# A softmax denominator's folded sum, split into a high and a low half and multiplied with ones in two rounded products

## The chip, the cores and the metric

The kernel runs on one core of one Trainium2 chip. The metric is the time of one execution on the device, in microseconds (us); a run's figure is the median of its executions. The engines are PE (TensorE, matrix products), DVE (VectorE), ACT (ScalarE), POOL (GpSimd) and SP (SyncE, which issues transfers).

## The reference, cut to what matters

An encoder layer. Its first attention path has 8 query heads in 2 groups of 4, sweeps all 2048 keys, and is an ordinary softmax:

```
s = jnp.einsum('bkgqd,bksd->bkgqs', qblk, k).astype(jnp.float32) * scale
p = jax.nn.softmax(s, axis=-1).astype(v.dtype)
return jnp.einsum('bkgqs,bksd->bkgqd', p, v)
```

For each query the kernel needs the weighted sum of the values and the sum of the 2048 exponentials, the denominator. Around it lie the input projection (stage 1), a windowed attention (3), the output projection (4) and a feed-forward net (5, 6).

## The kernel before, in words

The six stages run one after the other, each a block of its own with a barrier at its end. Stage 2, `attend_global` (L476 to L817), is the one that the change is in. It runs over 32 **groups** n: 8 heads times 4 chunks of 512 queries. A group is cut into 8 **units** u of 256 keys. Products use the rounded 32-bit type F32R, and where precision is needed a value is split in a rounded high part and a low rest. In the trace a unit is this:

- PE, `scores` (L766, L767): four products fill two of the four banks of `s_ps`; units alternate between the two pairs of banks, so `scores(u)` waits until DVE has finished the low part of unit u-2. Then `max_products` (L749) for the next group: two products into `m_ps`, which wait for DVE's last reduction. Then `weigh` (L781, L790) for unit u-2: two products with the high part, two with the low part. Unit 7 is also summed on PE (L784).
- ACT, `exponentials` (L676, L677): `p_hi`, the rounded exponential, and then the unrounded one in place.
- DVE, `low` (L720): `p_lo` = unrounded less rounded, for unit u-1; then `reduce` (L704): the running maximum for the next group. At u = 4 the eighth reduction of a group is followed by L708 and L711, which make the negated maximum `neg_max`.
- POOL: adds `p_hi` of units 0 to 6 up into `p_sum`, 128x1024 (L644, six adds), then folds the two halves of 512 together (L648). After the add of u = 4 it also runs `combine` for the group before (L630 and L634, 64x512 each), which puts two parts of the output together.

The order on each engine is the order of the program text, written out by hand; nothing is planned at run time. `total(n - 1)` (L794 to L796) is what turns the folded `p_sum` into the denominator: one product with the constant `ones_high`, in plain fp32, into a spare row of `ob_ps` of the group that runs then. PE issues it at the end of u = 4 of group n:

```
if u == 4 and n > 0:
    total(n - 1, False)
```

After the last group `total(31)` stands alone and ends the stage, followed by a copy on ACT (L697) and the stores. `ob_ps` itself is copied out by ACT in `keep_b` (L665) after u = 1 of the next group, `oa_ps` by `keep_a` (L658).

Semaphores of a stage can be used again by later stages. Those of stage 1 are collected in a list, `scratch["project_sems"]`, and POOL clears them one by one at the start of stage 4 (L1335, L1336); it then waits for the first `scale_heads` (L1347).

Of the kernel before, what the change touches and what calls it, by code (L numbers as in the profile page):

```python
# [21 lines left out]
F32 = mybir.dt.float32  # L22
F32R = mybir.dt.float32r
# [4 lines left out]
P = 128  # L28
# [103 lines left out]
def project(nc, a, scratch):  # L132
    with ExitStack() as ctx:
# [35 lines left out]
        qk_ps = ps("qk_ps", [P, 12, P])  # L169

        def sem(name):
            scratch["project_sems"].append(ctx.enter_context(nc.semaphore(name)))
            return scratch["project_sems"][-1]

        const_in = sem("const_in")
        gains_in = sem("gains_in")
# [299 lines left out]
def attend_global(nc, a, scratch):  # L476
# [11 lines left out]
    ADDS = BY_ADDS  # L488
    ONE_LOW, ONE_HIGH = HD, HD + 32
    with ExitStack() as ctx:  # L490
        sb, ps, sem = make_alloc(nc, ctx)
        kt = sb("kt", [P, NG, 2, SEQ], F32R)
        v = sb("v", [P, NT, NG, 2 * HD], F32R)
        v_one = sb("v_one", [P, NT, NG, 2 * HD], F32R)
# [10 lines left out]
        o_down = sb("o_down", [P, 2, QB])  # L505
        o_half = sb("o_half", [P, QB])
        o_sum = sb("o_sum", [P, 2, QB])
        ones_high = sb("g_ones_high", [P, 2 * HD])
        ones_low = sb("g_ones_low", [P, 2 * HD], F32R)
        s_ps = ps("s_ps", [P, 4, NB])  # L510
        m_ps = ps("m_ps", [P, 2, NB])
# [12 lines left out]
        scores_ready, p_hi_ready, probs_ready = sem("g_scores_ready"), sem("g_p_hi_ready"), sem("g_probs_ready")  # L524
        p_lo_ready, added = sem("g_p_lo_ready"), sem("g_added")
        high_used, low_used, sum_used = sem("g_high_used"), sem("g_low_used"), sem("g_sum_used")
        oa_kept, ob_kept = sem("g_oa_kept"), sem("g_ob_kept")
        shifted = [sem(f"g_shifted{s}") for s in range(2)]
        summed = sem("g_summed")
# [82 lines left out]
        @block.gpsimd  # L612
        def _(pool):
            nc.gpsimd.memset(kt[HD:HD + 1, :, 1, :].bitcast(F32), 1.0).then_inc(filled, 1)
            pool.drain()
            nc.gpsimd.memset(v_one[:, :, :, HD:ONE_HIGH].bitcast(F32), 1.0)
            pool.drain()
            nc.gpsimd.memset(v_one[:, :, :, ONE_HIGH:].bitcast(F32), 0.0).then_inc(filled, 1)
            pool.drain()
            nc.gpsimd.memset(ones_high[:, 0:ONE_HIGH], 0.0)  # L620
            pool.drain()
            nc.gpsimd.memset(ones_high[:, ONE_HIGH:], 1.0)
            nc.gpsimd.memset(ones_low[:].bitcast(F32), 0.0)
            pool.drain()
            nc.gpsimd.memset(ones_low[:, ONE_LOW:ONE_HIGH].bitcast(F32), 1.0).then_inc(filled, 1)

            def combine(n):
                s = n % 2
                pool.wait_ge(shifted[s], 16 * (n // 2 + 1))
                nc.gpsimd.tensor_tensor(o_half[0:HD], o_a[0:HD, s], o_down[0:HD, s], ALU.add)  # L630
                pool.wait_ge(ob_kept, n + 1)
                at_least(pool, o_stored[s], 16 * (n // 2))
                pool.drain()
                nc.gpsimd.tensor_tensor(o_sum[0:HD, s], o_half[0:HD], o_b[0:HD, s], ALU.add).then_inc(summed, 1)  # L634

            for n in range(TOTAL):
                s = n % 2
                for u in range(1, BY_ADDS):
                    pool.drain()
                    if u == 1:  # L640
                        at_least(pool, sum_used, n - 1)
                    pool.wait_ge(p_hi_ready, UNITS * n + u + 1)
                    first = p_hi[:, (UNITS * n) % SLOTS].bitcast(F32) if u == 1 else p_sum[:, s]
                    nc.gpsimd.tensor_tensor(p_sum[:, s], first, p_hi[:, (UNITS * n + u) % SLOTS].bitcast(F32), ALU.add).then_inc(added, 1)  # L644
                    if u == 4 and n > 0:
                        combine(n - 1)
                pool.drain()
                nc.gpsimd.tensor_tensor(p_sum[:, s, 0:QB], p_sum[:, s, 0:QB], p_sum[:, s, QB:], ALU.add).then_inc(added, 1)  # L648
            combine(TOTAL - 1)

        @block.scalar
        def _(act):
            def keep_a(n):
                s = n % 2
                act.wait_ge(high_used, UNITS * (n + 1))
                at_least(act, summed, n - 1)
                at_least(act, shifted[s], 16 * (n // 2))
                nc.scalar.activation(o_a[:, s], oa_ps[:], ACT.Copy).then_inc(oa_kept, 1)  # L658

            def keep_b(n):  # L660
                s = n % 2
                act.wait_ge(low_used, UNITS * (n + 1))
                at_least(act, summed, n - 1)
                at_least(act, den_stored[s], 32 * (n // 2) - (16 if s == 0 else 0) if n > 1 else 0)
                nc.scalar.activation(o_b[:, s], ob_ps[:], ACT.Copy).then_inc(ob_kept, 1)  # L665

            def exponentials(n, u):
                at = UNITS * n + u
                slot = at % SLOTS
                scored = s_ps[:, 2 * (u % 2):2 * (u % 2) + 2].rearrange("p b c -> p (b c)")  # L670
                act.wait_ge(scores_ready, at + 1)
                at_least(act, high_used, at - SLOTS + 1)
                before = at - SLOTS
                if at >= SLOTS and before % UNITS < BY_ADDS:
                    act.wait_ge(added, ADDS * (before // UNITS) + max(before % UNITS, 1))
                nc.scalar.activation(p_hi[:, slot], scored, ACT.Exp).then_inc(p_hi_ready, 1)  # L676
                nc.scalar.activation(scored, scored, ACT.Exp).then_inc(probs_ready, 1)  # L677

            def copy_v(g):
                act.wait_ge(v_loaded[g], 16)  # L680
                nc.scalar.activation(v_one[:, :, g, 0:HD], v[:, :, g, 0:HD].bitcast(F32), ACT.Copy).then_inc(v_copied, 1)

            copy_v(0)
            for n in range(TOTAL):
                for u in range(UNITS):
                    if u == 4 and n % ITER == ITER - 2 and n // ITER + 1 < NG:
                        copy_v(n // ITER + 1)
                    exponentials(n, u)
                    if u == LAG - 1 and n > 0:
                        keep_a(n - 1)  # L690
                        keep_b(n - 1)
            keep_a(TOTAL - 1)
            keep_b(TOTAL - 1)
            act.wait_ge(sum_used, TOTAL)
            act.wait_ge(den_stored[TOTAL % 2], 32 * (TOTAL // 2) - 16)
            act.wait_ge(summed, TOTAL - 1)
            nc.scalar.activation(o_b[:, TOTAL % 2], ob_ps[:], ACT.Copy).then_inc(ob_kept, 1)  # L697

        @block.vector
        def _(dve):  # L700
            def reduce(n, m):
                products = first_bank(m) if n == 0 else m_ps[:]
                dve.wait_ge(max_product, PAIRS * n + m + 1)
                nc.vector.tensor_reduce(part_max[:, m // (PAIRS // QT), m % (PAIRS // QT):m % (PAIRS // QT) + 1],  # L704
                                        products.rearrange("p b c -> p (b c)"), AX, ALU.max).then_inc(max_reduced, 1)
                if m == PAIRS - 1:
                    nc.vector.drain()
                    nc.vector.tensor_reduce(row_max[:], part_max[:], AX, ALU.max)  # L708
                    nc.vector.drain()
                    at_least(dve, max_placed[n % 2], 16 * QT * (n // 2))  # L710
                    nc.vector.tensor_scalar(neg_max[:, n % 2], row_max[:], -1.0, None, ALU.mult).then_inc(max_ready, 1)  # L711

            def low(n, u):
                at = UNITS * n + u
# [11 lines left out]
            for n in range(TOTAL):  # L726
                for u in range(UNITS):
                    if n > 0 or u > 0:
                        low(n if u else n - 1, (u - 1) % UNITS)
                    ahead, m = pair_of(n, u)  # L730
                    if ahead < TOTAL:
                        reduce(ahead, m)
            low(TOTAL - 1, UNITS - 1)

        @block.tensor
        def _(pe):
# [55 lines left out]
                last.then_inc(low_used, 1)  # L792

            def total(n, alone):  # L794
                pe.wait_ge(added, ADDS * (n + 1))
                nc.tensor.matmul(ob_ps[:], ones_high[:], p_sum[:, n % 2, 0:QB], start=alone, stop=alone).then_inc(sum_used, 1)  # L796

            for m in range(PAIRS):
                max_products(0, m)
# [3 lines left out]
            for n in range(TOTAL):  # L803
                for u in range(UNITS):
                    at = UNITS * n + u
                    scores(n, u)
                    ahead, m = pair_of(n, u)
                    if ahead < TOTAL:
                        max_products(ahead, m)
                    if at >= LAG:  # L810
                        weigh((at - LAG) // UNITS, (at - LAG) % UNITS)
                    if u == 4 and n > 0:
                        total(n - 1, False)
            for u in range(UNITS - LAG, UNITS):
                weigh(TOTAL - 1, u)
# [405 lines left out]
def mix_heads(nc, a, scratch):  # L1221
    with ExitStack() as ctx:
# [109 lines left out]

        @block.gpsimd
        def _(pool):
            for done in scratch["project_sems"]:  # L1335
                pool.sem_clear(done)  # L1336
            nc.gpsimd.memset(half[:], -0.5)
            pool.drain()
# [590 lines left out]
def build(nc, a, out, upto=6, kind="Internal"):  # L1929
    def dram(name, shape):  # L1930
        return nc.dram_tensor(name, shape, F32, kind=kind).ap()

    scratch = {
        "project_sems": [],
        "q_t": dram("q_turned", [HEADS // 2, P, SEQ]),
        "k_t": dram("k_turned", [NG, P, SEQ]),
        "v_glob": dram("v_glob", [NT, P, NG, 2 * HD]),
# [62 lines left out]
```

## Time and profile before

| what | value |
|---|---|
| median of 3 runs | 2890.35 us (2888.19 to 2890.84) |
| the profiled execution: its own time | 2890.22 us |
| the profiled execution: its span, first to last instruction | 2888.6 us |
| busy in the span: PE, DVE, ACT, POOL | 2705.4, 1827.9, 1429.2, 803.3 us |
| stage 2: its groups run | about 372 to 1046 us of the span |
| granted PE clock, mean | 0.972 of full speed (1.00 in the groups of stage 2) |

The profile is of one execution. Busy time is the time in which an engine had an instruction running; an instruction that is held up by another engine after it was started counts as busy. "Idle before" names the instruction that ended an engine's wait, as inferred from semaphores. The span leaves out 1.6 us around the first and the last instruction.

### The profile page before, as it was taken

How to read it: one execution, taken by the hardware profiler on the slowest of the kernel's cores; microseconds unless marked ns; L12 is line 12 of the kernel's file. 1: busy time of each engine (PE TensorE's matmuls, PEld its weight loads, DVE VectorE, ACT ScalarE, POOL GpSimd, SP SyncE). 2: the span in 40 equal slices, each digit the busy share in tenths (PEclk: the TensorE clock that was granted, in tenths of full speed). 3: DMA queues.
4: the chain of work that ended last, by engine and by line, in shares of the span. 5: the costliest groups of instructions: out<-in, count | busy, mean ns of one | idle time of the engine just before them, and what ended most of it. 6: DMA issues, size and time to landing. Idle time of an engine off the chain costs nothing. (4 is left out here: it accounts for less than half of the span.)

```text
span 2888.6 us, 36041 instructions
## 1 busy us (share of the span) xinstructions
PE 2705.4 (94%) x12274; PEld 2185.6 (76%) x12274; DVE 1827.9 (63%) x2503; ACT 1429.2 (49%) x2122; POOL 803.3 (28%) x603
## 2 busy tenths in 40 slices
PE   7999599999999978988995999999998999999998
PEld 5888467777777747976874888788886888888887
DVE  5666499999999947865556666675653343343433
ACT  3222177777777747973334544554443333233332
POOL 1111178888888854541110000000000000000000
PEclk9999799999999989998997999999999999999999
DMA  5333421111111122327876333533325445355442
GB/s 181 107 108 102 122 67 30 31 34 28 35 30 32 23 75 70 84 67 218 207 202 216 124 117 97 209 107 100 114 92 189 171 172 182 121 196 179 172 172 98
DMA packets 295611, 338.16 MB, mean 117 GB/s; under 512 B 73059, under 2 KB 219635, under 8 KB 293292
## 3 DMA queue, kind: packets, MB, share of 16 engines
q1 hardware_dynamic: 269980, 317.92, 35.7%
q10 hardware_dynamic: 23552, 13.64, 1.5%
q0 software_dynamic: 1936, 4.74, 0.6%
q8 instruction: 84, 1.38, 0.2%
q14 instruction: 59, 0.48, 0.0%
HBM read 234.10 MB, written 97.86 MB: 115 GB/s over the span
## 5 line engine op out<-in xcount | busy, mean ns | idle before, releaser
L126 PE MATMUL d_pr<-d_w_hi,d_s_hi 128*128 128x512 f32 x1024 | 399.7, 390 | 11.6 <-DVE d_s_lo L1872 11.6
L1871 DVE TENSOR_TENSOR d_w_lo<-d_w_raw,d_w_hi 128x1024 fp32r<-128x1024 f32 x128 | 156.8, 1225 | 386.2 <-ACT d_s_hi L1848 382.3
L127 PE MATMUL d_pr<-d_w_lo,d_s_hi 128*128 128x512 f32 x1024 | 399.5, 390 | 0.0
L128 PE MATMUL d_pr<-d_w_hi,d_s_lo 128*128 128x512 f32 x1024 | 399.3, 390 | 0.0
L644 POOL TENSOR_TENSOR p_sum<-p_sum,p_hi 128x1024 f32<-128x1024 f32 x160 | 383.3, 2396 | 37.0 <-issue 19.7
L126 PE MATMUL u_pr<-u_t_hi,u_w_hi 128*128 128x512 f32 x896 | 351.2, 392 | 32.3 <-DVE u_t_lo L1687 31.9
L127 PE MATMUL u_pr<-u_t_lo,u_w_hi 128*128 128x512 f32 x896 | 350.1, 391 | 0.0
L128 PE MATMUL u_pr<-u_t_hi,u_w_lo 128*128 128x512 f32 x896 | 350.1, 391 | 0.0
L676 ACT ACTIVATE p_hi<-s_ps 128x1024 fp32r<-128x1024 f32 x256 | 263.3, 1028 | 157.0 <-PE s_ps L767 155.7
L720 DVE TENSOR_TENSOR p_lo<-s_ps,p_hi 128x1024 fp32r<-128x1024 f32 x256 | 312.5, 1221 | 29.5 <-ACT s_ps L677 22.3
L704 DVE TENSOR_REDUCE part_max<-m_ps 128x1 f32<-128x1024 f32 x251 | 304.6, 1214 | 33.1 <-PE m_ps L749 32.9
L1846 ACT ACTIVATE d_w_hi<-d_w_raw 128x1024 fp32r<-128x1024 f32 x128 | 135.6, 1060 | 271.0 <-PE d_pr L128 181.3
L677 ACT ACTIVATE s_ps<-s_ps 128x1024 f32<-128x1024 f32 x256 | 261.4, 1021 | 0.0
L766 PE MATMUL s_ps<-q_all,kt 128*128 128x512 f32 x512 | 219.1, 428 | 18.3 <-DVE p_lo L720 18.2
L126 PEld LDWEIGHTS d_pr<-d_w_hi,d_s_hi 128*128 128x128 f32 x1024 | 192.9, 188 | 52.2 <-DVE d_s_lo L1872 12.1
L128 PEld LDWEIGHTS d_pr<-d_w_hi,d_s_lo 128*128 128x128 f32 x1024 | 193.0, 188 | 40.2
L127 PEld LDWEIGHTS d_pr<-d_w_lo,d_s_hi 128*128 128x128 f32 x1024 | 193.0, 188 | 40.0
L126 PEld LDWEIGHTS u_pr<-u_t_hi,u_w_hi 128*128 128x128 f32 x896 | 169.2, 189 | 70.4 <-issue 34.4
L1630 ACT ACTIVATE u_pr<-u_pr 128x512 f32<-128x512 f32 x128 | 74.5, 582 | 273.4 <-DVE u_pr L1716 126.7
L767 PE MATMUL s_ps<-q_max,kt 65*128 65x512 f32 x512 | 203.9, 398 | 0.0
L1839 POOL TENSOR_TENSOR d_rstd<-d_var,d_half 128x1 f32<-128x1 f32 x16 | 8.8, 550 | 699.7 <-DVE d_var L1879 699.7
L127 PEld LDWEIGHTS u_pr<-u_t_lo,u_w_hi 128*128 128x128 f32 x896 | 169.3, 189 | 35.2
(219 smaller groups left out, 5384.5 us busy)
## 6 DMA issues: line engine op xcount, KB each, us to landing
d_w_raw<-in_w_ffn_down SPq DMA_DIRECT2D x128, 512.0 KB, 3.8
u_w_raw<-in_w_ffn_up SPq DMA_DIRECT2D x32, 1024.0 KB, 6.0
act_blocks<-u_s_out SPq DMA_DIRECT2D x128, 256.0 KB, 6.2
d_s_lo<-act_blocks SPq DMA_DIRECT2D x128, 256.0 KB, 2.7
u_t_lo<-h_blocks SPq DMA_DIRECT2D x14, 1024.0 KB, 10.9
x_in<-in_x SPq DMA_DIRECT2D x16, 512.0 KB, 4.3
q_split<-q_out ACTq DMA_DIRECT2D x16, 512.0 KB, 3.3
q_turned<-w_raw SPq DMA_DIRECT2D x16, 512.0 KB, 3.4
```

The lines of the kernel that those rows point to most:

```text
L126: nc.tensor.matmul(out, stat_hi, mov_hi, start=first, stop=False)
L127: nc.tensor.matmul(out, stat_hi, mov_lo, start=False, stop=False)
L128: return nc.tensor.matmul(out, stat_lo, mov_hi, start=False, stop=last)
L644: nc.gpsimd.tensor_tensor(p_sum[:, s], first, p_hi[:, (UNITS * n + u) % SLOTS].bitcast(F32), ALU.add).then_inc(added, 1)
L676: nc.scalar.activation(p_hi[:, slot], scored, ACT.Exp).then_inc(p_hi_ready, 1)
L677: nc.scalar.activation(scored, scored, ACT.Exp).then_inc(probs_ready, 1)
L704: nc.vector.tensor_reduce(part_max[:, m // (PAIRS // QT), m % (PAIRS // QT):m % (PAIRS // QT) + 1], products.rearrange("p b c -> p (b c)") ...
L720: nc.vector.tensor_tensor(p_lo[:, slot], scored, p_hi[:, slot].bitcast(F32), ALU.subtract).then_inc(p_lo_ready, 1)
L766: nc.tensor.matmul(bank, kt[:, g, 0, keys], q_all[:, n % QS], start=True, stop=False)
L767: last = nc.tensor.matmul(bank, kt[0:HD + 1, g, 1, keys], q_max[0:HD + 1, n % QS], start=False, stop=True)
L1846: nc.scalar.activation(w_hi[:, n % SLOTS], w_raw[:, n % RAW], ACT.Copy)
L1871: nc.vector.tensor_tensor(w_lo[:, n % SLOTS], w_raw[:, n % RAW], w_hi[:, n % SLOTS].bitcast(F32), ALU.subtract)
```

## The change

Three things. First, `total` becomes two F32R products. ACT makes `sum_hi`, the rounded `p_sum[:, :, 0:512]`; DVE makes `sum_lo`, the rest; PE multiplies `ones_high`, now F32R too, with the one and then the other, in the same accumulation. Second, where each piece stands in its engine's order: `sum_high(n-1)` on ACT after the exponentials of u = 3, `sum_low(n-1)` on DVE at the end of u = 4, `total(n-1)` on PE at the end of u = 6 instead of u = 4; all three once more, one after the other, behind the last group. Third, stage 2's semaphores join the list that POOL clears in stage 4, and the list has a new name.

```diff
         def sem(name):
-            scratch["project_sems"].append(ctx.enter_context(nc.semaphore(name)))
-            return scratch["project_sems"][-1]
+            scratch["early_sems"].append(ctx.enter_context(nc.semaphore(name)))
+            return scratch["early_sems"][-1]
...
-        sb, ps, sem = make_alloc(nc, ctx)
+        sb, ps, _ = make_alloc(nc, ctx)
+
+        def sem(name):
+            scratch["early_sems"].append(ctx.enter_context(nc.semaphore(name)))
+            return scratch["early_sems"][-1]
+
...
-        ones_high = sb("g_ones_high", [P, 2 * HD])
+        ones_high = sb("g_ones_high", [P, 2 * HD], F32R)
+        sum_hi = sb("g_sum_hi", [P, QB], F32R)
+        sum_lo = sb("g_sum_lo", [P, QB], F32R)
...
+        sum_hi_made, sum_lo_made = sem("g_sum_hi_made"), sem("g_sum_lo_made")
...
+            def sum_high(n):
+                act.wait_ge(added, ADDS * (n + 1))
+                at_least(act, sum_used, n)
+                nc.scalar.activation(sum_hi[:], p_sum[:, n % 2, 0:QB], ACT.Copy).then_inc(sum_hi_made, 1)
+
...
                     exponentials(n, u)
+                    if u == 3 and n > 0:
+                        sum_high(n - 1)
                     if u == LAG - 1 and n > 0:
                         keep_a(n - 1)
                         keep_b(n - 1)
             keep_a(TOTAL - 1)
             keep_b(TOTAL - 1)
+            sum_high(TOTAL - 1)
             act.wait_ge(sum_used, TOTAL)
...
+            def sum_low(n):
+                dve.wait_ge(sum_hi_made, n + 1)
+                nc.vector.tensor_tensor(sum_lo[:], p_sum[:, n % 2, 0:QB], sum_hi[:].bitcast(F32), ALU.subtract).then_inc(sum_lo_made, 1)
+
...
                     if ahead < TOTAL:
                         reduce(ahead, m)
+                    if u == 4 and n > 0:
+                        sum_low(n - 1)
             low(TOTAL - 1, UNITS - 1)
+            sum_low(TOTAL - 1)
...
             def total(n, alone):
-                pe.wait_ge(added, ADDS * (n + 1))
-                nc.tensor.matmul(ob_ps[:], ones_high[:], p_sum[:, n % 2, 0:QB], start=alone, stop=alone).then_inc(sum_used, 1)
+                pe.wait_ge(sum_lo_made, n + 1)
+                nc.tensor.matmul(ob_ps[:], ones_high[:], sum_hi[:], start=alone, stop=False)
+                nc.tensor.matmul(ob_ps[:], ones_high[:], sum_lo[:], start=False, stop=alone).then_inc(sum_used, 1)
...
-                    if u == 4 and n > 0:
+                    if u == 6 and n > 0:
                         total(n - 1, False)
...
-            for done in scratch["project_sems"]:
+            for done in scratch["early_sems"]:
                 pool.sem_clear(done)
```

The memsets of `ones_high` (L620, L622) get a bitcast to fp32 and are otherwise as before. Nothing outside these lines changes.

## Rows read from the trace of the kernel before

**Rows 1.** Groups of instructions by line, stage 2 (372 to 1050 us); columns as in the page.

```profile
L711 DVE TENSOR_SCALAR neg_max<-row_max 128x4 fp32r<-128x4 f32 x31 | 48.3, 1559 | 2.7 <-issue 0.4
...
L796 PE MATMUL ob_ps<-p_sum,g_ones_high 128*128 128x512 f32 x64 | 32.9, 595 | 2.0 <-POOL p_sum L648 2.0
...
L658 ACT ACTIVATE o_a<-oa_ps 128x512 f32<-128x512 f32 x32 | 18.9, 590 | 0.8 <-PE ob_ps L784 0.8
```

**Rows 2.** Waits, stage 2: who waited for whom; us in total, times, longest.

```profile
PEld s_ps L766 <- DVE p_lo L720: 32.1, 35, 1.5
```

**Rows 3.** Timeline of PE, one group: start, duration in us, line, xcount, [idle before].

```profile
721.17 0.50 PE L766 MATMUL s_ps<-q_all,kt 128*128 128x512 f32 x1 [0.50 <-DVE p_lo L720]
...
732.14 0.40 PE L767 MATMUL s_ps<-q_max,kt 65*128 65x512 f32 x1
...
738.59 1.02 PE L796 MATMUL ob_ps<-p_sum,g_ones_high 128*128 128x512 f32 x2
739.04 0.80 PE L766 MATMUL s_ps<-q_all,kt 128*128 128x512 f32 x1
739.68 0.39 PE L767 MATMUL s_ps<-q_max,kt 65*128 65x512 f32 x1
...
741.32 0.62 PE L790 MATMUL ob_ps<-p_lo,v_one 128*128 128x512 f32 x2
...
742.37 0.50 PE L766 MATMUL s_ps<-q_all,kt 128*128 128x512 f32 x1 [0.43 <-DVE p_lo L720]
```

**Rows 4.** Timeline of ACT, the same group.

```profile
732.58 1.03 ACT L676 ACTIVATE p_hi<-s_ps 128x1024 fp32r<-128x1024 f32 x1
...
737.21 1.03 ACT L676 ACTIVATE p_hi<-s_ps 128x1024 fp32r<-128x1024 f32 x1 [0.39 <-PE s_ps L767]
```

**Rows 5.** Timeline of POOL, the same group.

```profile
730.79 2.40 POOL L644 TENSOR_TENSOR p_sum<-p_hi 128x1024 f32<-128x1024 f32 x1 [1.62 <-ACT p_hi L676]
733.68 2.41 POOL L644 TENSOR_TENSOR p_sum<-p_sum,p_hi 128x1024 f32<-128x1024 f32 x1 [0.50 <-ACT p_hi L676]
...
738.80 2.37 POOL L644 TENSOR_TENSOR p_sum<-p_sum,p_hi 128x1024 f32<-128x1024 f32 x1 [0.16 <-issue]
741.13 1.28 POOL L630 TENSOR_TENSOR o_half<-o_a,o_down 64x512 f32<-64x512 f32 x1
```

**Rows 6.** Timeline of DVE, the same group.

```profile
739.59 1.60 DVE L711 TENSOR_SCALAR neg_max<-row_max 128x4 fp32r<-128x4 f32 x1
741.11 1.21 DVE L720 TENSOR_TENSOR p_lo<-s_ps,p_hi 128x1024 fp32r<-128x1024 f32 x1
```

**Rows 7.** Line L368 (stage 1): count, duration in ns min/median/max, first and last start.

```profile
L368 DVE TENSOR_TENSOR q_out<-proj,q_out x16: 691/692/693, 47.4 to 319.3; 128x512 f32<-128x512 f32 x16
```

**Rows 8.** Line L1460 (stage 4), in the same columns.

```profile
L1460 DVE TENSOR_TENSOR m_x<-m_x,m_y x16: 1224/1226/1526, 1329.6 to 1515.5; 128x1024 f32<-128x1024 f32 x16
```

**Rows 9.** Timelines of POOL and DVE in stage 4, where two operations meet.

```profile
1352.59 1.29 POOL L1347 TENSOR_TENSOR m_hn<-m_sums,m_scales 128x512 f32<-128x512 f32 x1 [0.64 <-DMA m_scales<-rden]
...
1353.43 1.53 DVE L1460 TENSOR_TENSOR m_x<-m_x,m_y 128x1024 f32<-128x1024 f32 x1 [0.16 <-issue]
```

**Rows 10.** Timeline of stage 1 near 46 us, where two others meet.

```profile
45.81 2.96 POOL L330 TENSOR_TENSOR head_rstd<-head_var,half 128x10 f32<-128x10 f32 x1 [1.81 <-DVE head_var L383]
...
47.37 0.69 DVE L368 TENSOR_TENSOR q_out<-proj,q_out 128x512 f32<-128x512 f32 x1
```

**Rows 11.** Timeline of the end of stage 2.

```profile
1045.20 1.26 POOL L648 TENSOR_TENSOR p_sum<-p_sum 128x512 f32<-128x512 f32 x1 [0.16 <-issue]
...
1046.42 1.26 POOL L630 TENSOR_TENSOR o_half<-o_a,o_down 64x512 f32<-64x512 f32 x1
...
1046.61 1.25 PE L796 MATMUL ob_ps<-p_sum,g_ones_high 128*128 128x512 f32 x2 [2.05 <-POOL p_sum L648]
```

**Rows 12.** Line L1336 (stage 4): POOL's queue clears the semaphores of stage 1.

```profile
L1336 POOLq EVENT_SEMAPHORE_RANGE_CLEAR  x32: 44/44/48, 1292.7 to 1294.9; - x32
```

**Rows 13.** Timeline of POOL, start of stage 4.

```profile
1303.06 1.26 POOL L1347 TENSOR_TENSOR m_hn<-m_sums,m_scales 128x512 f32<-128x512 f32 x1 [7.97 <-DMA m_scales<-rden]
```

More of the change, by code:

```diff
@@ L619, in _ @@
             pool.drain()
-            nc.gpsimd.memset(ones_high[:, 0:ONE_HIGH], 0.0)
+            nc.gpsimd.memset(ones_high[:, 0:ONE_HIGH].bitcast(F32), 0.0)
             pool.drain()
-            nc.gpsimd.memset(ones_high[:, ONE_HIGH:], 1.0)
+            nc.gpsimd.memset(ones_high[:, ONE_HIGH:].bitcast(F32), 1.0)
             nc.gpsimd.memset(ones_low[:].bitcast(F32), 0.0)
@@ L1933, in build @@
     scratch = {
-        "project_sems": [],
+        "early_sems": [],
         "q_t": dram("q_turned", [HEADS // 2, P, SEQ]),
```

## The prediction

> **What bounds the kernel now.** I read the page first: PE is busy nearly all the time, so it looks as if any microsecond taken from PE were a microsecond won. That is an average over six stages, so I went on to the stage of the change: its groups by line, its waits, and then the timeline of one group, engine by engine. Two rows do not fit a stage bound by PE. PE's weight loads stand waiting for the low part that DVE makes, 32.1 us in 35 waits, about one us in each group [rows 2]. And DVE's tiny `neg_max` operation, 128x4, takes 1.56 us on average [rows 1].
>
> The timeline explains both. L711 starts at 739.59 and ends at 741.19 [rows 6]; POOL's add of unit 4 ends at 741.17 [rows 5]. The tiny operation is held until POOL's add is over. Behind it stands `low(4)`, 741.11 to 742.32 [rows 6], and PE's scores of unit 6, which wait for it, start at 742.37 [rows 3]. Followed backwards this closes into a loop, and the reader is to see that each piece starts as the one before it ends:
>
> - PE, scores of unit 6 (721.17) through to the last score of unit 2 of the next group (732.14 + 0.40 = 732.54) [rows 3]: 11.37 us;
> - ACT, `p_hi` of unit 2: 732.58 to 733.61 [rows 4];
> - POOL, the adds of units 2, 3 and 4: 733.68 to 741.17 [rows 5]: 7.5 us;
> - DVE, the held L711 and `low(4)`: to 742.32 [rows 6];
> - PE again at 742.37, 21.20 us after 721.17 [rows 3].
>
> So a group's 21.2 us is set by this loop, not by PE's sum. PE's old `total`, at 738.59, lies in the part that the loop does not use: PE has run out of work by about 741.8 (two products of 0.62 from 741.32, the last 0.39 of which runs beside a follower) and idles, 0.43 us by the row, until 742.37 [rows 3].
>
> **The change part by part.**
>
> *PE loses the plain fp32 product.* It shows as two instructions of 595 ns [rows 1]. From its start at 738.59 to the third product behind it at 739.68 are 1.09 us; a stream of rounded products advances by 0.62 - 0.39 = 0.23 us each [rows 3]. The pair thus holds PE for 1.09 - 0.23 = 0.86 us. It goes from u = 4, and I cost that at **0**: what covers it is the wait for `low(4)`, which only gets longer. Were the cover gone (no wait for DVE in a group), it would be worth 0.86.
>
> *PE gains two rounded products at u = 6*: 2 x 0.23 = **+0.46 us**. That place is in the loop, between unit 6 and unit 7. `sum_lo` is long made by then, so no wait comes with it. Bounds: 0 (if PE had a gap there after all) and 0.86 (if they cost as the old pair).
>
> *ACT gains `sum_high` after u = 3*: 0.59 us, taken from L658 [rows 1], the fold that it reads being done before 730.79, when the next group's first add starts [rows 5]. It falls into a wait of 0.39 us before `p_hi(4)` [rows 4], so that comes at most 0.2 us later, at 738.4; POOL's add of unit 4 starts at 738.80 [rows 5] and DVE's `low(4)` at 741.11. Cost **0**; with that cover gone 0.2.
>
> *DVE gains `sum_low` right behind L711*, ahead of `low(4)`: in the loop. Alone a 128x512 subtraction with both operands in SBUF takes 0.69 us [rows 7], and DVE starts the next 0.08 before the end of the last (741.19 against 741.11 [rows 6]): 0.61. But it does not stand alone. POOL went straight on to `combine`, L630, at 741.13 [rows 5]. What happens when DVE wants two SBUF operands while POOL runs such an operation is seen in stage 4: L1460, 1.23 us as a rule [rows 8], takes 1.53 when it starts inside L1347 [rows 9]. POOL's operation ended at 1353.88, DVE's at 1354.96, that is 1.23 after 1353.73: DVE was held until 0.15 before POOL's recorded end. So `sum_low` is held until 741.13 + 1.28 - 0.15 = 742.26, ends at 742.95, and `low(4)` starts at 742.87 instead of 741.11: **+1.76 us**. Bounds: 0.61, not held; and held over L634 as well, another 1.42 (its 1.28 and 0.14 between the two): 3.18. I take 1.76, since L1347 and L630 are alike (a tensor operation over 512 columns), and L1460 was held by one operation only.
>
> The Trainium skill ("SBUF — State Buffer", Who interferes with whom) says that such a pair of ports is locked by whoever starts first, for its whole instruction. The rows agree for L1347 but not everywhere: L368, also with two SBUF operands, took its usual 0.69 at 47.37, in the midst of a POOL operation of 2.96 us [rows 10, 7]. By the rule the term is 1.76 as well; by the second row it would be 0.61, which is the first rival below.
>
> *What follows in a group.* The `low(4)` delay moves PE's unit 6, and the products at its end move unit 7. POOL's L634 starts up to half a us later; POOL has 1.62 us to spare before the next group's first add [rows 5]. DVE's reductions keep their distance to PE. Period: 21.2 + 1.76 + 0.46 = 23.4 us. L711 and `sum_low` meet in groups 1 to 30: 30 x 2.22 = **66.6 us**. In group 31 there are no reductions; DVE has gaps, and `sum_low` can fit before `low(4)`: 0, at most one POOL add of 2.4.
>
> *The end of the stage.* Now PE starts the last product at 1046.61 behind the fold and ends at 1047.86 [rows 11]. After the change: ACT 0.59 from 1046.5; DVE could start at 1047.1 but L630 runs until 1047.68 [rows 11], so held until 1047.53, to 1048.22; then two rounded products, 0.05 + 0.62, to 1048.9. The range is +0.4 to +1.7, taken **+1.0**.
>
> *Semaphores.* POOL cleared 32 in 2.2 us from 1292.7 [rows 12]; stage 2 adds 36 (34 and the two new ones), 36 x 0.07 = 2.5 us, to 1297.5. POOL's next operation that matters waits for a transfer until 1303.06 [rows 13]: **0**. With that cover gone it would be 2.5.
>
> Sum: 66.6 + 1.0 = 67.6 on the profiled execution's 2890.2, which lies 0.1 from the median: **2958 us**.
>
> **The rivals.**
>
> 1. *`sum_low` is not held*, or takes the ports before L630 does. For: [rows 10], and L630 touches only 64 partitions. Against: [rows 9], and L630 has started when L711 ends. Then 0.61 + 0.46 = 1.07 a group, 32 us, and about 0.7 at the end: 2923.
> 2. *`sum_low` is held over L630 and L634.* For: both are of one kind and 0.14 us apart. Against: L711 gets in between two POOL operations [rows 5, 6], and its mean of 1.56 says that it does so nearly every time [rows 1]. 3.18 + 0.46 = 3.64, times 30: 109 + 1: 3000.
> 3. *Faster: PE decides after all.* Place: the stretch from unit 7 to unit 5, if the loop above is a coincidence of equal lengths. Then the pair's 0.86 becomes 0.46 and 31 groups win 0.4 each: 12 us, 2878. It decides only from the point where `low(4)` is ready before PE has finished unit 5, about 741.8; it is ready at 742.32 without `sum_low`. Every group shows such a wait, which speaks against it.
> 4. *No change*: the saving on PE and the 0.61 on DVE both vanish in gaps, 2891. It needs a `sum_low` that runs within L711's held time, yet the order of the program puts it behind. That the split does nothing at all is not open: the products change type and number.
>
> **How the numbers follow.** Forecast 0.67, rival 1 0.16, rival 2 0.07, rival 3 0.05, rival 4 0.05. The forecast's own range is 2944 (the 0.46 is not in the loop) to 2966. The wanted 8 in 10 is reached with rival 1 and the forecast, with the bounds of the end and of group 31 on top: 2920 to 2972. A difference of about 0.2% (6 us) is what a measurement of this kernel can tell from none. Faster 0.05, the same 0.05, slower 0.90.
>
> **What would show it.** In the changed profile: `sum_low` as a row of some 1.8 us, not 0.69, ending half a us and more after L630; PE's wait for DVE before unit 6 near 3 us instead of 0.5 to 1; the group's period 23.4 us; the total pair at 0.62; L711 still near 1.56; L634 beginning late or lasting longer; ACT's `sum_high` before a wait that shrinks. A `sum_low` row of 0.69 is rival 1; one of 3.3, rival 2. A period under 21.2 would mean that the loop was misread.

## The result, and the profile after

The changed kernel takes 2967.67 us (2964.64 to 2967.82, four runs), the kernel before 2890.6 us: a ratio of 1.0266 with a 95% interval of 1.0249 to 1.0282, that is 77 us slower. Its profiled execution took 2967.53 us, with a span of 2965.8 us. The forecast was 2958 us with a range of 2920 to 2972. The time lies in the range, but the sum behind it does not hold: its largest term, `sum_low`, came out 1.16 us a group too large, and a term of about 1.5 us a group, the clock of PE, was missing.

The loss is in stage 2. From the first to the last copy of `oa_ps`, 31 groups, it took 651.7 us before and 729.2 after. The groups of the changed kernel, by line (what was L711 is L727, L630 is L638; L731 is `sum_low`, L690 `sum_high`, L819 and L820 the two products):

```profile
L638 POOL TENSOR_TENSOR o_half<-o_a,o_down 64x512 f32<-64x512 f32 x31 | 54.8, 1766 | 0.0
L727 DVE TENSOR_SCALAR neg_max<-row_max 128x4 fp32r<-128x4 f32 x31 | 50.0, 1612 | 2.4
...
L731 DVE TENSOR_TENSOR g_sum_lo<-p_sum,g_sum_hi 128x512 fp32r<-128x512 f32 x31 | 21.9, 705 | 0.0
...
L690 ACT ACTIVATE g_sum_hi<-p_sum 128x512 fp32r<-128x512 f32 x31 | 19.2, 618 | 0.0
...
L819 PE MATMUL ob_ps<-g_sum_hi,g_ones_high 128*128 128x512 f32 x31 | 18.9, 611 | 0.0
```

`sum_low` takes 0.705 us on average, 0.68 in each of 30 groups, not the 1.8 of the forecast: there it is not held. The one exception is group 31, where no held L727 stands before it: it starts inside a POOL add and takes 1.51. L638, POOL's operation beside it, has gone from 1.28 us to 1.77. And the product L819 takes 611 ns where a rounded product of 512 columns takes some 390.

The waits of stage 2 answer to [rows 2]:

```profile
PEld s_ps L789 <- DVE p_lo L740: 77.1, 36, 2.9
```

Now a group at the hand-over from DVE to PE. First the timeline of POOL, then that of DVE, then that of PE; they answer to [rows 5], [rows 6] and [rows 3].

```profile
732.37 2.39 POOL L652 TENSOR_TENSOR p_sum<-p_sum,p_hi 128x1024 f32<-128x1024 f32 x1 [0.16 <-issue]
734.72 1.78 POOL L638 TENSOR_TENSOR o_half<-o_a,o_down 64x512 f32<-64x512 f32 x1
```

```profile
733.20 1.59 DVE L727 TENSOR_SCALAR neg_max<-row_max 128x4 fp32r<-128x4 f32 x1
734.70 0.68 DVE L731 TENSOR_TENSOR g_sum_lo<-p_sum,g_sum_hi 128x512 fp32r<-128x512 f32 x1
735.30 1.21 DVE L740 TENSOR_TENSOR p_lo<-s_ps,p_hi 128x1024 fp32r<-128x1024 f32 x1
```

```profile
734.00 0.61 PE L813 MATMUL ob_ps<-p_lo,v_one 128*128 128x512 f32 x2
736.57 0.50 PE L789 MATMUL s_ps<-q_all,kt 128*128 128x512 f32 x1 [1.96 <-DVE p_lo L740]
736.91 0.40 PE L790 MATMUL s_ps<-q_max,kt 65*128 65x512 f32 x1
...
737.79 1.19 PE L772 MATMUL m_ps<-kt,q_all 128*128 128x512 f32 x2
738.78 1.05 PE L804 MATMUL oa_ps<-p_hi,v 128*128 128x512 f32 x2
739.63 1.05 PE L813 MATMUL ob_ps<-p_lo,v_one 128*128 128x512 f32 x2
740.49 0.63 PE L819 MATMUL ob_ps<-g_sum_hi,g_ones_high 128*128 128x512 f32 x1
...
741.19 0.39 PE L789 MATMUL s_ps<-q_all,kt 128*128 128x512 f32 x1
```

The reader is to see two things. L727 is held by POOL's add and ends with it (734.79 and 734.76), and `sum_low` follows it at once, with its usual length. POOL's next operation is the one that is late: L638 is recorded from 734.72 to 736.50, and 736.50 less its usual 1.28 is 735.22, which is 0.16 before the end of `sum_low`. I read this as L638 waiting for `sum_low`. So DVE loses 0.60 us here, not 1.76. And PE has waited from 734.46, when the next product could have started (734.00 and two advances of 0.23), to 736.57. That is 2.1 us; the row says 1.96, since it counts from the end of the last product. The texts of the experiments count such gaps the first way, the rows the second. After the wait PE runs its first four products at 0.23 us each and the next eight, from 737.79 to 741.19, at 0.43: 3.40 us where eight products at 0.23 take 1.84. That is 1.56 us lost to the clock of PE.

That the clock is what changed is seen in the granted clock, first of three microseconds in the midst of the slow products, then of two groups in turn. Columns: stretch, length, busy us (x instructions) of PE, PEld, DVE, ACT and POOL, granted clock, share and GB/s of transfers.

```profile
738.00:741.00 3.00, 3.00 (x8) 2.32 (x9) 2.75 (x3) 1.77 (x2) 2.76 (x2) 0.50 0.22 44
```

```profile
400.35:422.65 22.30, 20.35 (x86) 15.43 (x85) 21.04 (x19) 16.99 (x19) 18.72 (x10) 1.00 0.44 102
422.65:446.40 23.75, 21.80 (x86) 16.51 (x85) 21.09 (x19) 16.97 (x19) 18.68 (x10) 0.93 0.14 29
```

The two groups hold the same instructions. The earlier one, the first with a `sum_low`, took 22.30 us at full clock, and 21.2 + 0.60 + 0.46 is 22.26. From the next on the clock falls to its lower level (0.50, that is 1.2 of 2.4 GHz) for a part of each group, and nearly every group takes 23.75 to 23.9. So the 77.5 us of the 31 groups are about 32 for the two operations (30 x 1.06: 0.60 for `sum_low`, 0.46 for the total in the loop) and about 45 for the clock (29 groups of 1.56). The end of the stage adds 1.7. Against that, the stages behind it took 3.2 us less in this execution than before (1837.5 and 1840.7), which the change does not explain.

The end of the stage and the semaphores:

```profile
1123.93 1.26 POOL L656 TENSOR_TENSOR p_sum<-p_sum 128x512 f32<-128x512 f32 x1 [0.16 <-issue]
1125.15 1.26 POOL L638 TENSOR_TENSOR o_half<-o_a,o_down 64x512 f32<-64x512 f32 x1
...
1125.89 1.07 DVE L731 TENSOR_TENSOR g_sum_lo<-p_sum,g_sum_hi 128x512 fp32r<-128x512 f32 x1 [4.03 <-ACT g_sum_hi L690]
...
1127.67 0.63 PE L820 MATMUL ob_ps<-g_sum_lo,g_ones_high 128*128 128x512 f32 x1
```

```profile
L1360 POOLq EVENT_SEMAPHORE_RANGE_CLEAR  x68: 44/44/48, 1371.8 to 1376.8; - x68
```

Behind the last group `sum_low` starts 0.74 us after L638, and here it is held: 1.07 us, 0.39 more than alone. From the fold's end (1125.19) to the last product's (1128.30) are 3.1 us, before it was 1.4 [rows 11]. The 68 clears end at 1376.8, and POOL's next waits for a transfer until 1382.7: hidden, as forecast.

### The profile page after: what moved, and what is told of

Its sections match the earlier page's. It is cut to its first block and busy times, and to the rows that moved or that the text cites. A ratio compares the mean times of both kernels' runs of the same rounds, so it can differ in the third digit from the quotient of the medians.

```text
span 2965.8 us, 36172 instructions
## 1 busy us (share of the span) xinstructions
PE 2738.5 (92%) x12274; PEld 2219.9 (75%) x12274; DVE 1855.1 (63%) x2535; ACT 1442.4 (49%) x2154; POOL 818.2 (28%) x603
## 5 line engine op out<-in xcount | busy, mean ns | idle before, releaser
L789 PE MATMUL s_ps<-q_all,kt 128*128 128x512 f32 x512 | 207.5, 405 | 62.2 <-DVE p_lo L740 62.2
L772 PE MATMUL m_ps<-kt,q_all 128*128 128x512 f32 x502 | 181.5, 445 | 21.2 <-DMA kt<-k_turned 14.8
```

The lines of the kernel that those rows point to most:

```text
L772: last = nc.tensor.matmul(bank[:, e], q_all[:, n % QS, t * P:(t + 1) * P], kt[:, n // ITER, 0, (c + e) * NB:(c + e + 1) * NB], start=True, ...
L789: nc.tensor.matmul(bank, kt[:, g, 0, keys], q_all[:, n % QS], start=True, stop=False)
```

## The experiments

Theory G: the loop (PE's unit 6 to unit 2, ACT, POOL's adds, held `neg_max`, `low(4)`, PE) sets the group; `sum_low` puts 0.60 into it, the total 0.46, and the wait of 2.1 us that PE now has before unit 6 lowers PE's clock, another 1.5 or so. Its first rival, S: the slow products come from the new operations themselves. The later letters stand for rivals that the expectations below state: P and N on how POOL holds DVE (e6), F and D on what bounds e8 (e9).

| run | time, us | ratio to before, 95% | a group, us |
|---|---|---|---|
| the change | 2967.7 | 1.0249 to 1.0282 | 23.8 to 23.9 |
| e1, total at u = 5 | 2913.5 | 1.0054 to 1.0090 | 21.83 (23.4 in 2 groups) |
| e2, gap filled | 2926.6 | 1.0106 to 1.0142 | 22.3 |
| e3, halves made, not used | 2908.6 | 1.0044 to 1.0080 | 21.8 |
| e4, plain total at u = 6 | 2928.4 | 1.0108 to 1.0144 | 22.1 or 23.7 |
| e6, the change, no held `neg_max` | 2962.2 | 1.0233 to 1.0268 | 23.8 (22.2 in 2 groups) |
| e5, before, no held `neg_max` | 2859.9 | 0.9880 to 0.9913 | 20.27 |
| e7, split early | 2889.5 | 0.9985 to 1.0004 | 21.2 |
| e8, split early, no held `neg_max` | 2890.5 | 0.9988 to 1.0007 | 21.22 |
| e9, split in u = 1 and 2, no held `neg_max` | 2865.2 | 0.9895 to 0.9928 | 20.4 |

**e1: the total in the gap.**

```diff
-                    if u == 6 and n > 0:
+                    if u == 5 and n > 0:
                         total(n - 1, False)
```

> The changed kernel with the two products of the total at the end of u = 5 instead of u = 6. Theory G (the gap in PE before unit 6, 2.1 us long, lowers PE's granted clock, and this costs 1.5 of the 2.56 us per group; sum_low costs 0.60, the total in the loop 0.46): the products now fall into the gap and split it, the clock stays at 1.00, and a group takes 21.2 + 0.6 = 21.8 us: 2909 us. Theory S (the slow products behind unit 6 come from the new operations themselves, by contention or by the tiles they read, whatever the gap): 23.3 us a group, 2953 us.

Measured: 2913.5 us; one moved line gives back 54 of the 77 us. The timeline of PE shows why:

```profile
465.59 0.61 PE L813 MATMUL ob_ps<-p_lo,v_one 128*128 128x512 f32 x2
467.01 0.50 PE L819 MATMUL ob_ps<-g_sum_hi,g_ones_high 128*128 128x512 f32 x1 [0.81 <-DVE g_sum_lo L731]
467.35 0.40 PE L820 MATMUL ob_ps<-g_sum_lo,g_ones_high 128*128 128x512 f32 x1
468.15 0.50 PE L789 MATMUL s_ps<-q_all,kt 128*128 128x512 f32 x1 [0.40 <-DVE p_lo L740]
...
469.37 1.19 PE L772 MATMUL m_ps<-kt,q_all 128*128 128x512 f32 x2
```

The two products stand in the middle of the old gap. Most groups take some 21.8 us. But the rows shown are from one of the two that took 23.4: with both waits short, the clock fell there all the same. The shorter waits of this run make the fall rare, they do not rule it out.

**e2: useless work in the gap.** The tile `nothing` is new and holds zeros.

```diff
+                    if u == 5 and n > 0:
+                        for _ in range(6):
+                            nc.tensor.matmul(oa_ps[:], nothing[:], q_all[:, n % QS], start=False, stop=False)
                     if u == 6 and n > 0:
                         total(n - 1, False)
```

> The changed kernel with six more products at the end of u = 5, of a tile of zeros, added to oa_ps: 1.4 us of useless work inside PE's gap of 2.1 us. Theory G: the clock stays at 1.00, a group takes 21.2 + 0.60 + 0.46 = 22.3 us, and the kernel gets faster by added work: 2924 us. Theory S: the products behind unit 6 stay slow, no gain: 2967 us.

Measured: 2926.6 us, 41 us faster than the change, by six products of zeros in each group. Nothing else was moved, the split and the total stand where the change has them. Two groups in a row, in the columns used above:

```profile
690.50:735.20 44.70, 43.03 (x180) 32.89 (x180) 42.26 (x37) 34.35 (x39) 37.51 (x19) 1.00 0.14 30
```

```profile
714.66 1.56 PE L840 MATMUL oa_ps<-q_all,g_nothing 128*128 128x512 f32 x6
716.77 0.50 PE L791 MATMUL s_ps<-q_all,kt 128*128 128x512 f32 x1 [0.55 <-DVE p_lo L742]
```

The clock is 1.00 and a group takes 22.3 us. S falls: the new operations are all there, no product is slow.

**e3: the halves made and not used.** PE keeps the plain product at u = 4, with `ones_high` in plain fp32 again; `sum_high` and POOL wait for `sum_low` to be through where they waited for the product alone.

```diff
-                pe.wait_ge(sum_lo_made, n + 1)
-                nc.tensor.matmul(ob_ps[:], ones_high[:], sum_hi[:], start=alone, stop=False)
-                nc.tensor.matmul(ob_ps[:], ones_high[:], sum_lo[:], start=False, stop=alone).then_inc(sum_used, 1)
+                pe.wait_ge(added, ADDS * (n + 1))
+                nc.tensor.matmul(ob_ps[:], ones_high[:], p_sum[:, n % 2, 0:QB], start=alone, stop=alone).then_inc(sum_used, 1)
...
-                    if u == 6 and n > 0:
+                    if u == 4 and n > 0:
                         total(n - 1, False)
```

> sum_hi and sum_lo are made as in the changed kernel, but not used: PE makes the one plain fp32 product at u = 4 as before. Theory G: only sum_low is in the loop, 21.2 + 0.6 = 21.8 us a group, 2909 us; PE's gap is 0.66 + 0.60 = 1.3 us, and whether the clock stands that is open (if not, up to 1.5 more a group, 2953). Had sum_low been held as predicted: 1.76, 2943 us with a sum_low row of 1.8 us. Theory S (contention of sum_low with PE): slow products, 2950 us or so, with a gap too short to matter.

Measured: 2908.6 us and 21.8 us a group, none of them slow, `sum_low` 0.68 in 30 groups. The subtraction alone is 0.6 us a group and 18 us in all.

**e4: the plain product late**, in the kernel before, with nothing new in it.

```diff
-                    if u == 4 and n > 0:
+                    if u == 6 and n > 0:
                         total(n - 1, False)
```

> The kernel before with its one plain fp32 product moved from u = 4 to the end of u = 6 and nothing else. 0.86 us of PE's work go into the loop: 21.2 + 0.86 = 22.1 us a group, 2916 us; the gap before unit 6 grows to 0.66 + 0.86 = 1.5 us. Theory G allows the clock to fall here (up to 1.5 us more a group, 2961 us) if 1.5 us of gap do what 2.1 do. Theory S says 2916 us with no slow product, since no new operation is there.

Measured: 2928.4 us, between the two numbers, and the groups show why: 18 take about 22.1 us and 11 about 23.7. Two neighbours:

```profile
672.87:696.60 23.73, 22.39 (x86) 16.31 (x85) 20.42 (x19) 17.38 (x19) 18.12 (x10) 0.93 0.13 28
696.60:718.40 21.80, 20.45 (x85) 15.23 (x83) 20.27 (x17) 16.57 (x19) 17.89 (x10) 1.00 0.14 32
```

```profile
675.65 0.50 PE L766 MATMUL s_ps<-q_all,kt 128*128 128x512 f32 x1 [1.34 <-DVE p_lo L720]
...
699.38 0.50 PE L766 MATMUL s_ps<-q_all,kt 128*128 128x512 f32 x1 [1.34 <-DVE p_lo L720]
```

PE's wait before unit 6 is 1.34 us by the row in both (a gap of 1.5, counted the other way), and only one loses clock. So the clock term is not a new operation's price, it comes with an idle PE. By the waits of the rows, 29 of 30 groups lose clock with 1.94 us (the change), 27 of 29 with 1.87 (e6), 11 of 29 with 1.34, none with 1.08 (e3), and 2 of 30 with the split wait of e1, 0.81 and 0.40. The move alone also shows that taking 0.86 us from u = 4 is worth nothing: a fast group is 0.86 us longer, not equal.

Next, POOL and DVE. **e6: the change without the held operation.** One reduction writes the negated maximum.

```diff
-                    nc.vector.tensor_reduce(row_max[:], part_max[:], AX, ALU.max)
-                    nc.vector.drain()
                     at_least(dve, max_placed[n % 2], 16 * QT * (n // 2))
-                    nc.vector.tensor_scalar(neg_max[:, n % 2], row_max[:], -1.0, None, ALU.mult).then_inc(max_ready, 1)
+                    nc.vector.tensor_reduce(neg_max[:, n % 2], part_max[:], AX, ALU.max, negate=True).then_inc(max_ready, 1)
+                    nc.vector.drain()
```

> The changed kernel, with the maximum's negation made in the reduction itself (one 128x4 reduction writes neg_max), so that the operation that waited for POOL is gone and sum_low comes on DVE while POOL's add of unit 4 is running. Theory P (a DVE operation with two SBUF operands is held by a POOL operation that is running, and was free in the changed kernel only because it came right behind the held one, ahead of POOL's next): sum_low is now held for 1.3 us or so, its row is about 2.0 us, low(4) starts where it did, and nothing is won: 23.8 us a group, 2966 us. Theory N (such an operation is not held in this stage): sum_low takes 0.68, low(4) starts 1.4 us earlier, PE's gap and with it the slow clock go: 20.5 us a group, 2870 us.

Measured: 2962.2 us. POOL and DVE in one group:

```profile
729.26 2.40 POOL L652 TENSOR_TENSOR p_sum<-p_sum,p_hi 128x1024 f32<-128x1024 f32 x1 [0.16 <-issue]
731.63 1.71 POOL L638 TENSOR_TENSOR o_half<-o_a,o_down 64x512 f32<-64x512 f32 x1
```

```profile
729.86 0.16 DVE L725 TENSOR_REDUCE neg_max<-part_max 128x4 fp32r<-128x8 f32 x1
730.11 2.10 DVE L730 TENSOR_TENSOR g_sum_lo<-p_sum,g_sum_hi 128x512 fp32r<-128x512 f32 x1
732.14 1.21 DVE L739 TENSOR_TENSOR p_lo<-s_ps,p_hi 128x1024 fp32r<-128x1024 f32 x1
```

Theory P holds, N falls. `sum_low` now takes 2.10 us: it has inherited the wait of `neg_max`. It ends at 732.21, 0.68 after 731.53, which is 0.13 before the add's recorded end at 731.66. The prediction's rule holds here, its use did not: an operation of DVE is held by one of POOL that is running, but which of two waiting ones goes first was not seen in any row of before. Here as in the change it was DVE's in 30 of 30 groups, and POOL's L638 took longer (1.71 us).

**e5: the kernel before without the held operation.** The same edit, in the kernel before.

> The kernel before with the negation inside the reduction and nothing else. If the loop over POOL's adds, the held neg_max and low(4) is what sets a group (the prediction's reading), then the link is cut and PE's own sum is left: 82 products of 0.23 and 0.86 for the total, 19.9 us, and some 0.2 of small waits: 20.1 us a group, 2857 us. If PE was the bound all along and the held operation was only idle time, 21.2 us and 2890.

Measured: 2859.9 us, 1.0% faster than before (0.9880 to 0.9913). PE in 100 us of it:

```profile
600.00:700.00 100.00, 100.00 (x416) 76.70 (x415) 94.04 (x85) 82.06 (x91) 89.66 (x46) 1.00 0.16 34
```

The loop of the prediction was the bound: with the loop cut at `neg_max`, PE is busy throughout, at 20.27 us a group. This kernel has the lowest time here.

**e7: the split early**, all else as in the change.

```diff
-                    if u == 3 and n > 0:
+                    if u == 0 and n > 0:
                         sum_high(n - 1)
...
                         low(n if u else n - 1, (u - 1) % UNITS)
+                    if u == 1 and n > 0:
+                        sum_low(n - 1)
...
-                    if u == 4 and n > 0:
-                        sum_low(n - 1)
...
-                    if u == 6 and n > 0:
+                    if u == 4 and n > 0:
                         total(n - 1, False)
```

> The changed kernel with sum_high after the exponentials of u = 0, sum_low between low(0) and the reduction of u = 1, and the total at u = 4 as in the kernel before. The split then lies outside the loop and the total in the part of PE that has slack: a group as before, 21.2 to 21.4 us, PE's gap before unit 6 about 1.1 us and the clock kept: 2890 to 2898 us. If sum_low costs 0.6 wherever it stands because DVE is full: 21.8 us, 2909.

Measured: 2889.5 us over ten runs, a ratio of 0.9985 to 1.0004: no difference from before. The same arithmetic as in the change, at places outside the loop, costs nothing and wins nothing. It has next to no slack there, though, in the rows of POOL and ACT:

```profile
708.14 1.29 POOL L656 TENSOR_TENSOR p_sum<-p_sum 128x512 f32<-128x512 f32 x1 [0.16 <-issue]
```

```profile
709.46 0.63 ACT L690 ACTIVATE g_sum_hi<-p_sum 128x512 fp32r<-128x512 f32 x1
```

The fold that `sum_high` reads ends at 709.43, 0.03 us before ACT comes to it. That matters in the next run.

**e8: both.** The edits of e7 and e6 together.

> Both: the early split of the run before, and the negation inside the reduction. With the loop cut, PE's sum decides, and there the two rounded products are worth 0.4 us a group less than the plain one: 19.5 and some waits, 19.7 us a group, 2845 us, 12 us under the kernel before with the negation alone. If DVE, with 0.6 us more, becomes the bound instead: 20.0 us or more, no faster than that one.

A miss: 2890.5 us, 45 over the expectation. DVE is not full, it is busy in 91.17 of 100 us (600 to 700). The waits say what happened, and the timelines of ACT and POOL where:

```profile
ACT g_sum_hi L690 <- POOL p_sum L656: 36.3, 30, 1.7
```

```profile
708.15 0.63 ACT L690 ACTIVATE g_sum_hi<-p_sum 128x512 fp32r<-128x512 f32 x1 [1.07 <-POOL p_sum L656]
708.69 1.01 ACT L684 ACTIVATE p_hi<-s_ps 128x1024 fp32r<-128x1024 f32 x1
```

```profile
706.83 1.29 POOL L656 TENSOR_TENSOR p_sum<-p_sum 128x512 f32<-128x512 f32 x1 [0.16 <-issue]
709.84 2.40 POOL L652 TENSOR_TENSOR p_sum<-p_hi 128x1024 f32<-128x1024 f32 x1 [1.72 <-ACT p_hi L684]
```

In e7 the fold was done just as ACT came to it. With the first loop cut, ACT comes to it earlier, and `sum_high` waits 1.07 us for the fold with `p_hi(1)` behind it, for which POOL waits in turn: 1.72 us from the fold's end to the next add. With POOL's six adds, `combine` and fold that closes a second loop, at 21.22 us as long as the first; nothing here shows more than coincidence in that.

**e9: the second loop opened.** `sum_high` behind the exponentials of u = 1, `sum_low` behind `low(1)`:

```diff
-                    if u == 0 and n > 0:
+                    if u == 1 and n > 0:
                         sum_high(n - 1)
...
-                    if u == 1 and n > 0:
+                    if u == 2 and n > 0:
                         sum_low(n - 1)
```

> As the run before (e8) but with sum_high on ACT behind the exponentials of u = 1 and sum_low on DVE behind low(1), in u = 2; negation inside the reduction, total at u = 4. Theory F (in e8 ACT waits for POOL's fold, and that closes a new loop: fold, sum_high, p_hi(1), POOL's next adds, 21.2 us): p_hi(1) no longer stands behind the fold, the loop is open, and a group takes 20.3 to 20.6 us if sum_low falls between two of POOL's adds: 2862 to 2872 us. If sum_low is instead held by the add of u = 1 or 2 and DVE becomes the bound: 21 us or more, 2885 us and up, with sum_low rows over 1 us. Theory D (DVE is full with 0.7 us more, and e8 was bound by that): 21.2 us again, 2890 us, with sum_low rows of 0.69 and no idle time on DVE.

Measured: 2865.2 us, 20.4 us a group. F holds in the main and D falls: the loop is open, and DVE has no less to do than in e8. `sum_high` and `sum_low` were moved together, so the gain is not told apart between them. And `sum_low` does not fall between two adds, as F had it; it meets the tail of POOL's add:

```profile
715.35 2.40 POOL L652 TENSOR_TENSOR p_sum<-p_hi 128x1024 f32<-128x1024 f32 x1 [0.36 <-ACT p_hi L684]
```

```profile
717.35 0.95 DVE L730 TENSOR_TENSOR g_sum_lo<-p_sum,g_sum_hi 128x512 fp32r<-128x512 f32 x1
```

It is held 0.27 us, until 717.62, again 0.13 before the add's recorded end. That is the change's idea at its best place among those tried, and it wins nothing over e5, which has no split: it is 5 us longer, with ratios to before whose intervals overlap (0.9895 to 0.9928, and 0.9880 to 0.9913) and a group of 20.4 against 20.27. PE's two rounded products should save 0.4 us a group (0.86 less 0.46), and none of it arrives. PE is busy 99% instead of 100, which is too little to account for it; what bounds this kernel was not settled.

## Why the prediction was right or wrong

- *What bounds the kernel*: right. The loop over PE, ACT, POOL and DVE sets the group, not PE's sum. e5 cuts it and gains 31 us; the prediction's 21.2 us and the 20.1 that e5's text gives PE alone are 1.1 apart, and 0.95 was measured.
- *PE loses the plain product at u = 4, cost 0*: right in the first instance, e4 shows no gain from it. But the prediction said of this cover only that the wait "gets longer". A longer wait was the start of the largest term, and no price was put on it.
- *Two products at u = 6, 0.46*: right. 22.30 us in the first full group and about as much in e2, against 21.8 without them in e3.
- *`sum_high`, 0*: right. `p_hi(4)` starts at most 0.1 us later, and e3 leaves no room for a cost.
- *`sum_low`, 1.76*: **wrong**, it is 0.60 (e3, 0.68 alone less the overlap). The failed step is "POOL went straight on to `combine`", from which the prediction has `sum_low` held until L630 is through. That L630 starts right behind the add does not make POOL first to its operands: `sum_low` ran its usual 0.68 us in 30 of 30 groups, and L638 took 1.78 instead of 1.28. Where `sum_low` starts inside an operation of POOL it is held as the prediction says (e6 2.10, group 31 1.51, the end 1.07). The value was the lower bound of the range, and rival 1 named this very way ("or takes the ports before L630 does") at 0.16.
- *PE's clock*: **missing**. 1.56 us in 29 groups, 45 us in all, more than the other terms together. The prediction forecast a wait of PE near 3 us before unit 6 (it is 1.94 by the row) and listed it as a sign, without asking what PE does after such a wait. Rival 1's 2923 with this term added is 2968; rival 1 by itself falls 45 us short. That the sum came within 10 us of the result is luck: 1.16 us a group too much and about 1.5 too little.
- *The end, +1.0*: 1.7, the upper end. `sum_low` was held by L638 as described; PE's two products took 1.19 us instead of 0.67, at the low clock after 4.5 us of waiting.
- *Semaphores, 0*: right.
- *Rival 3, PE decides*: fallen, by e5. *Rival 2, two operations of POOL*: never seen. *Rival 4, no change*: fallen, by the result; the 0.60 on DVE does not vanish in a gap (e3).

The Trainium skill bears on both errors. The Trainium skill's page "SBUF — State Buffer" (Who interferes with whom) says that issue order decides who is blocked; in this case's rows DVE's operation is recorded 0.02 us before POOL's (734.70 and 734.72), which agrees, though the row alone would not let one foresee it. The Trainium skill's page "TensorE: Matmul & The Clock Gate" (HAM oscillation — how this bites in real kernels) describes a kernel whose PE starts each round at the low clock after waiting for a transfer. This case agrees in part: the granted clock falls in nearly every round, to 0.93 instead of 1.00 over a group, after waits for DVE of 1.94 us, but only behind the first four products. At the end of the stage, after a wait of 4.47 us, the granted clock is at 0.50 from the first product on, which agrees in full. The section points at the missing term, but it does not give its size.

## What to carry to other kernels

Before pricing an added operation, find the loop that sets the period, and ask of every engine off it what a longer wait does to it: here a wait of PE of 1.9 us in each round cost 1.56 us more in clock, one of 1.3 us did so in a part of the rounds, and a cheap filler, or the same work moved into the wait, bought most or all of it back. An operation of DVE with two SBUF operands, put behind one that waits for POOL, cost its own 0.6 us; with that one gone, it took over the wait (e6). Its price depends on what runs on POOL when its turn comes, not on its size alone. And when one loop is cut, look for the next one before adding up the gains (e8).

## What the runs showed that was not expected

- Six products of zeros, 1.4 us of PE's time in each group, made the changed kernel 41 us faster (e2).
- PE's clock went both ways with the same wait: in e4, 1.34 us before unit 6 in two neighbouring groups, one at 0.93 and one at 1.00. The first four products after the wait run fast even where the clock then falls. What decides between the two was not settled.
- DVE's operation wins against POOL's when both have waited for the same hand-over: 30 of 30 groups in the change, as L638's 1.78 us shows, and the same in e6 (1.71). It gets in 0.13 to 0.15 us before the recorded end of POOL's operation.
- The most useful edit here was not the change's: moving the negation into the reduction took away an operation that needs 0.17 us where nothing holds it and was recorded at 1.56 us on average, and 31 us went with it (e5).
